# Attention of a hybrid layer, reordered: one turn holds both heads of a pair and one query tile, heaviest tile first

## What is computed

```python
for blk in range(S // Q_BLOCK):
    t0 = blk * Q_BLOCK
    L = t0 + Q_BLOCK
    z = jnp.einsum('bhqd,bhkd->bhqk', qb, kb) * scale          # kb, vb: the first L rows
    mask = s_idx < t_idx
    log_keep = jnp.where(mask, jax.nn.log_sigmoid(-z), 0.0)
    suffix = lax.cumsum(shifted, axis=3, reverse=True)         # shifted: log_keep one to the left
    A = jnp.where(mask, jnp.exp(jax.nn.log_sigmoid(z) + suffix), 0.0)
    outs.append(jnp.einsum('bhqk,bhkd->bhqd', A, vb))
```

## Time and profile before

| | us |
|---|---|
| median of 3 runs | 1343.46 (1341.79 to 1344.67) |
| the profiled execution, its span | 1344.4 |
| attention stage in it | 116.0 to 546.6 |
| PE busy in 116 to 546 | 393.2 of 430 |
| DVE busy there | 200.1 |
| ACT busy there | 187.6 |

### The profile page before, as it was taken

How to read it: one execution, slowest core, us unless ns; L and a number is a source line. 1 busy time by engine, 2 the same in 40 slices (tenths; PEclk the granted TensorE clock), 3 DMA queues, 4 the chain that set the end, 5 groups by cost and what they waited for, 6 DMA issues and landing times. The chain is left out here.

```text
span 1344.4 us, 16647 instructions
## 1 busy us (share of the span) xinstructions
PE 1196.3 (89%) x5806; PEld 968.3 (72%) x5806; DVE 870.1 (65%) x910; ACT 732.0 (54%) x918; POOL 146.7 (11%) x193
## 2 busy tenths in 40 slices
PE   5999979969989997899837999999999999999930
PEld 4887767747767775688716888888888888888820
DVE  4414444435435453723166999999999999999926
ACT  4322534543454236211206888888888888888810
POOL 1000000000000003100010111111111111111000
PEclk9999989979999999899857999999999999999975
DMA  6111100100000003611155999999999999999409
GB/s 203 37 32 32 32 16 16 32 16 17 16 16 23 28 14 125 265 49 48 39 249 196 357 389 384 381 382 380 384 384 385 382 386 378 384 384 388 174 17 374
DMA packets 57338, 261.88 MB, mean 195 GB/s; under 512 B 13008, under 2 KB 33488, under 8 KB 43984
## 3 DMA queue, kind: packets, MB, share of 16 engines
q1 hardware_dynamic: 46928, 240.31, 46.9%
q0 software_dynamic: 9216, 16.80, 3.3%
q10 hardware_dynamic: 1152, 4.19, 0.8%
HBM read 252.88 MB, written 25.17 MB: 207 GB/s over the span
## 5 line engine op out<-in xcount | busy, mean ns | idle before, releaser
L1250 DVE TENSOR_TENSOR e_lo<-W,e_hi 128x1024 fp32r<-128x1024 f32 x384 | 452.6, 1221 | 25.6 <-ACT e_hi L1244 22.5
L1244 ACT ACTIVATE e_hi<-W 128x1024 fp32r<-128x1024 f32 x384 | 403.3, 1060 | 96.8 <-PE ps L1215 94.0
L735 DVE TENSOR_TENSOR_SCAN kept<-kept,start_at 128x128 f32<-128x128 f32 (+7 forms) x64 | 88.7, 1385 | 210.7 <-ACT kept L587 177.6
L1213 PE MATMUL ps<-e_hi,xT_hi 128*128 128x512 f32 x512 | 204.2, 399 | 7.1 <-DVE e_lo L1250 7.1
L1215 PE MATMUL ps<-e_lo,xT_hi 128*128 128x512 f32 x512 | 201.5, 394 | 0.0
L1214 PE MATMUL ps<-e_hi,xT_lo 128*128 128x512 f32 x512 | 201.0, 393 | 0.0
L406 PE MATMUL ps<-xnT_hi,w_hi 128*128 128x512 f32 x320 | 128.4, 401 | 15.2 <-DVE u L699 7.1
L586 ACT ACTIVATE soft<-ps,q_scale 128x127 f32<-128x127 f32 (+7 forms) x54 | 38.0, 704 | 186.4 <-PE ps L454 175.6
L406 PE MATMUL ps<-xnT_hi,w_lo 128*128 128x512 f32 x320 | 127.9, 400 | 0.0
L406 PE MATMUL ps<-xnT_lo,w_hi 128*128 128x512 f32 x320 | 127.7, 399 | 0.0
L1213 PEld LDWEIGHTS ps<-e_hi,xT_hi 128*128 128x128 f32 x512 | 97.6, 191 | 27.0 <-issue 4.0
(11 more groups left out here) (207 smaller groups left out, 1768.2 us busy)
## 6 DMA issues: line engine op xcount, KB each, us to landing
W<-in_w_dram SPq DMA_DIRECT2D x96, 2048.0 KB, 10.7
w_raw<-in_w_in_dram SPq DMA_DIRECT2D x20, 512.0 KB, 4.0
yy<-y_rows SPq DMA_DIRECT2D x8, 1024.0 KB, 13.6
xt<-in_x_dram SPq DMA_DIRECT2D x8, 512.0 KB, 3.8
w_out_raw<-in_w_out_dram SPq DMA_DIRECT2D x4, 1024.0 KB, 9.4
xn_rows<-xn SPq DMA_DIRECT2D x8, 512.0 KB, 2.6
out_dram<-x ACTq DMA_DIRECT2D x8, 512.0 KB, 9.0
x<-in_x_dram SPq DMA_DIRECT2D x1, 3072.0 KB, 14.9
```

What stands on the lines that cost most here:

```text
L735: dve.tensor_tensor_scan(back, back, one[:, ::-1], 0.0, ALU.mult, ALU.max).then_inc(multiplied, 1)
L1213: pe.matmul(o, xs_hi[:, k], e_hi[:, p, cols], start=(k == 0), stop=False)
L1244: act.activation(e_hi[:, p], flat[:, p * D:(p + 1) * D], ACT.Copy).then_inc(s["hi_made"], 1)
L1250: dve.tensor_tensor(e_lo[:, p], flat[:, p * D:(p + 1) * D], e_hi[:, p], ALU.subtract).then_inc(s["lo_made"], 1)
```

## The change

A unit becomes both heads of a pair and one query tile, so there are 32 units instead of 64, and within a pair the tile falls from 7 to 0. `scores` issues each of the three products for head 0 and head 1 in turn, into different PSUM banks; `values` issues each key tile's product for head 0 and head 1 in turn, into the two halves of the partitions of one bank. `probsT` gets a buffer for each head. `turn`, `open_unit`, `take_turned` and `weigh` take the head as an argument; PE runs turn(n, 0), a first share of projection, turn(n, 1), a second share. `open_unit` makes `kept` first, and the scan waits for that alone. Scores have two banks for each head (four), transposes two, value products bank 6, and projection groups after the first eight all use bank 7: a group starts when the group before has been read. DVE, not ACT, copies the "c" groups. The shares are 8 and 16 ticks in each unit of the first three pairs, and 24 and 24 in the first four units of the last, none in its last four. JOIN is unit 4 of 8 (5 in the last pair), and the scores of the unit after stand ahead of it.

```diff
-SHARE = (11, 11, 11, 11, 11, 11, 11, 11, 11, 20, 20, 11, 11, 11, 10, 10)
-SHARE_LAST = (16,) * 12 + (0,) * 4
+SHARE = ((8, 16),) * 8
+SHARE_LAST = ((24, 24),) * 4 + ((0, 0),) * 4
...
+        group_bank = lambda g: 6 + g % 2 if g < PRE_GROUPS else 7
-        JOIN = (9, 9, 9, 13)
-        length = lambda n: (n % PU // 2 + 1) * P
+        JOIN = (4, 4, 4, 5)
+        tile_of = lambda n: NT - 1 - n % NT
+        length = lambda n: (tile_of(n) + 1) * P
-        Z = lambda use: ps[:, use % 3]
-        TB = lambda g: ps[:, 3 + g % 2]
-        VB = 5
+        Z = lambda use, h: ps[:, 2 * h + use % 2]
+        TB = lambda g: ps[:, 4 + g % 2]
+        VB = 6
...
                 def project(first, last):
-                            if g >= 2:
+                            if PRE_GROUPS <= g:
+                                pe.wait_ge(bank_read[(g - 1) % 2], (g - 1) // 2 + 1)
+                            elif g >= 2:
                                 pe.wait_ge(bank_read[g % 2], g // 2)
...
                 def scores(n):
-                        pe.matmul(z, q_hi[p % 2][rows, cols], k_hi[p % 2][rows, c0:c1], start=True, stop=False)
-                        pe.matmul(z, q_hi[p % 2][rows, cols], k_lo[p % 2][rows, c0:c1], start=False, stop=False)
-                        mm = pe.matmul(z, q_lo[p % 2][rows, cols], k_hi[p % 2][rows, c0:c1], start=False, stop=True)
+                        pe.wait_ge(z_read, z_done[z_first[n] + hf - 2])
+                        for i, (qs, ks) in enumerate(((0, 0), (0, 1), (1, 0))):
+                            for h in range(2):
+                                rows = slice(h * HD, (h + 1) * HD)
+                                mm = pe.matmul(Z(z_first[n] + hf, h)[:, 0:c1 - c0], q2[qs][rows, cols], k2[ks][rows, c0:c1],
+                                               start=(i == 0), stop=(i == 2))
...
                 def values(n):
                     for j in range(t + 1):
-                        mm = pe.matmul(ps[h * HD:(h + 1) * HD, VB, (t % 4) * P:(t % 4 + 1) * P], v[:, j, head], probsT[:, j, :],
-                                       start=(j == 0), stop=(j == t))
+                        for h in range(2):
+                            head = slice((2 * p + h) * HD, (2 * p + h + 1) * HD)
+                            mm = pe.matmul(ps[h * HD:(h + 1) * HD, VB, (t % 4) * P:(t % 4 + 1) * P], v[:, j, head], probsT[h][:, j, :],
+                                           start=(j == 0), stop=(j == t))
...
                 for n in range(UNITS):
-                    p, r = divmod(n, PU)
-                    if r != JOIN[p] + 1 and n + 1 < UNITS:
+                    p, r = divmod(n, NT)
+                    if n + 1 < UNITS:
                         scores(n + 1)
-                    if n >= 2:
-                        values(n - 2)
                     if n:
-                        turn(n - 1)
-                    project(ticks_by(n - 1), ticks_by(n))
-                    if r == JOIN[p] and p + 1 < NPAIR:
-                        sums_of_qk(p + 1)
-                    if r == JOIN[p] + 1:
+                        values(n - 1)
+                    turn(n, 0)
+                    project(ticks_by(n, 0), ticks_by(n, 1))
+                    turn(n, 1)
+                    if r == JOIN[p]:
+                        if p + 1 < NPAIR:
+                            sums_of_qk(p + 1)
                         if p:
                             sums_of_rows(p)
-                        scores(n + 1)
+                    project(ticks_by(n, 1), ticks_by(n, 2))
...
                 def open_unit(n, h):
+                    act.activation(kept[h][:, S - L:], z, ACT.Sigmoid, scale=down).then_inc(kept_made, 1)
+                    act.activation(soft[h][:, S - L:S - 1], z[:, 0:L - 1], ACT.Sigmoid, scale=up).then_inc(z_read, halves(n))
...
+                    for h in range(2):
+                        take_turned(n, h)
+                        if n + 1 < UNITS:
+                            open_unit(n + 1, h)
```

More of the change, by code:

```diff
@@ L260, in hymba_moe_layer, with share, ticks_by @@
-        halves = lambda n: (length(n) + BANK - 1) // BANK
[L261 to L265, removed]
+        UNITS = NPAIR * NT
+        PRE_GROUPS = 2 * PRE
+        def share(n):
+            return (SHARE if n < UNITS - NT else SHARE_LAST)[n % NT]
+        def ticks_by(n, part):
+            return PRE_GROUPS * TICKS + sum(sum(share(m)) for m in range(n)) + sum(share(n)[:part])
@@ L266, in hymba_moe_layer @@
+        z_first, z_before, sum_qk, sum_rows, z_done = {}, {}, {0: 0}, {}, [1, 3]
+        for n in range(UNITS):
+            z_first[n], z_before[n] = len(z_done), z_done[-1]
+            z_done += [z_done[-1] + 2 * halves(n)] * halves(n)
+            p, r = divmod(n - 1, NT)
+            if n and r == JOIN[p]:
                 if p + 1 < NPAIR:
-                    sum_qk[p + 1] = z_uses
-                    z_uses += 3
+                    sum_qk[p + 1] = len(z_done)
+                    z_done += [z_done[-1] + 1, z_done[-1] + 3]
@@ L269, in hymba_moe_layer @@
                 if p:
[L270 to L274, removed]
[L275 to L281 removed]
+                    sum_rows[p] = len(z_done)
@@ L282, in hymba_moe_layer @@
+                    for _ in joint_rows[p]:
+                        z_done.append(z_done[-1] + 2)
+        Z = lambda use, h: ps[:, 2 * h + use % 2]
+        z_reads = lambda n, h: z_before[n] + (h + 1) * halves(n)
+        assert all(z_first[n] % 2 == 0 for n in range(UNITS) if halves(n) == 2)
+        th = lambda n, h: sum(2 * halves(m) for m in range(n)) + h * halves(n)
+        TB = lambda g: ps[:, 4 + g % 2]
+        VB = 6
         row_gain = lambda r: gain_conv[:, r:r + 1] if r < CB else gain_attn[:, r - CB:r - CB + 1]
@@ new lines, in scores @@
+                    for hf in range(halves(n)):
+                        c0, c1 = hf * BANK, min((hf + 1) * BANK, length(n))
+                        pe.wait_ge(z_read, z_done[z_first[n] + hf - 2])
[4 more added lines that the diff above has]
+                                               start=(i == 0), stop=(i == 2))
@@ L475, in _ @@
                 sums_of_qk(0)
[L476 removed]
+                project(5 * TICKS, PRE_GROUPS * TICKS)
                 pe.wait_ge(v_read, NT)
@@ L623, in _ @@
                 v_out(NT - 1)
-                for g in range(5):
+                for g in range(4):
                     take(g)
@@ L763, in _ @@
                 chunk_lo(3)
+                take(4)
                 scale_keys(0)
-                for g in range(4, 6):
-                    take(g)
+                take(5)
                 keys_lo(0)
```

203 lines of the change are left out of this document (93 added, 110 removed).

## The result

The changed kernel takes 1245.88 us in the median of four runs (1243.80 to 1248.69); the kernel before takes 1344.01 beside it. The ratio is 0.9269, 95% interval 0.9254 to 0.9284.

A forecast was written before the change was run, and what follows sets the result against it. The prediction took PE to bound the stage: 307.7 us of work, 34.2 idle and 8 for the clock make 350 instead of 430, 80 less, so 1264 us for the kernel, range 1247 to 1300.

The forecast's parts named there:

- the sum: PE's work in the stage from first score to last value copy: 377.4 us before, 307.7 after the change.
- Scores: 26.3 forecast: Score products of two heads, in different row halves, run together; their 52.6 us of PE fall by 26.3.
- Value products: 31.4 forecast: Value products of two heads, in different column halves, run together; their 62.8 us of PE fall by 31.4.
- one pair costs one: Two heads' products side by side take the time of one; taken as 26.3 us saved for scores, 31.4 for values.
- the row for two row halves: Profile row of the kernel before: both heads' first scores in merged pairs, 0.28 to 0.34 us long, like one alone.
- The load at 281.44: Head 0's weight load behind a join, ahead of head 1's 281.62 product; cited against strict program order for two row groups.
- Changes of kind: PE's extra time between kinds of product, about 0.50 us a unit: 32 us before, 12 saved by 32 units.
- the waits at the joins: PE idle at the joins for the open unit, table and Ln, and DVE's late copies: 14.6 of 34.2 us idle.
- table and Ln: PE waits at the joins for the open unit and ACT's table and Ln: 0.8, 2.4 and 2.4 us.
- DVE's copy of a projection group: In the second and third pair, key work, row scalings and head 1's scan delay it; PE waits about 4.5 us each.
- half clock: PE's loss to the granted clock in the stage: 8 us instead of 15.8, as fewer long gaps precede dense work.
- The end: Behind the last projection, tiles 3 to 0 are left: 26 us instead of 39, PE idle for 13 of them.

The follow-up runs named there:

- the three loads: The changed kernel with two more table loads at each join, 2.57 us of ACT each time; 1257.58 us, 0.9353 of the kernel before.

## Why the prediction was right and wrong

**PE's work: right.** PE's busy time at half clock, 5.02 us from 119 to 126 and 2.70 from 436 to 446, would be half of that at full clock, so half clock cost 3.9 us; 311.7 busy less 3.9 is 307.8, and the sum said 307.7. Scores: 26.3 forecast, 23.9 come back when pairing is taken away. Value products: 31.4 forecast, 29.5. Both bounds' choice of "one pair costs one" came out, and the row for two row halves carried over to two column halves; no row had shown the second, so it was a guess with a chance of its own against it. (Scores as priced add up to 52.3 us, not 52.6; it changes nothing.)

The tiling page's "Up to 2×" ("TensorEngine Tiling (Array Packing)", Theoretical Speedup, in the Trainium skill) agrees: 3.71 against 1.97 us. The rule of the Trainium skill's page "TensorE: Matmul & The Clock Gate", Part 3, that products start strictly in order and loads pass only in another row group, does not hold here: value products that share all rows pair in full, and by head they still pair at the seam. The load at 281.44 that the prediction set against this rule is no counterexample, since the rule lets a load of another row group pass; but the row above it does show one. Its x2 from 281.39 lasts 0.55 us, so it holds the product of that load, 0.49 long, from some 281.45 on, ahead of the products at 281.50 and 281.62 that come before it in the program.

**Changes of kind: right.** The unit above has 0.50 of them, and a second turn adds 0.08 (a first projection row of 0.47 instead of 0.39); 32 * 0.58 = 18.6 for the 20 in the sum.

**The step that failed: the waits at the joins.** I put 14.6 of the 34.2 us of idle time there. All idle time is 20.3, of which the start has 5.0 (4.22, 0.20, 0.54; forecast 6.6) and the end 12.6 (forecast 13), so joins and all between have 2.7. Two things were wrong in it. First, I had PE wait 2.4 us for table and Ln at the second and third join. At the second, ACT needs 3.6 us from PE's last transposes to the end of the Ln of q, and PE's own sums of q and k fill the same 3.6 (241.72 to 245.32). The prediction prices these sums rightly in PE's work (16 * 0.11 and 4 * 0.43, 3.5 us); it does not set them in full against the wait.

Second, I had PE wait 4.5 us for DVE's copy of a projection group in each of the second and third pair. The queue ahead of that copy stands there as I said it would. The changed kernel behind the second join, DVE, then PE's first projection product behind the next unit's transposes:

```profile
258.20 1.28 DVE L734 SCALAR_TENSOR_TENSOR y_mix<-y_mix,gain_attn 128x1024 f32<-128x1024 f32 x1
...
260.59 0.69 DVE L744 TENSOR_TENSOR_SCAN kept<-kept,start_at 128x256 f32<-128x256 f32 x1
...
261.66 0.69 DVE L708 TENSOR_TENSOR u<-ps,u 128x512 f32<-128x512 f32 x1
...
262.49 0.47 PE L417 MATMUL ps<-xnT_hi,w_hi 128*128 128x512 f32 x1
```

The copy is done at 262.35, and PE, which has the scores, value products and transposes of the next unit until 262.49, does not wait; the copy comes 0.14 us before it is needed. DVE can start that queue at 253.7 because it was free before: PE's sums make the group end later and the scores ahead of the join are open early, so DVE idles 7.5 us before the copy at 253.06. With the scores behind the sums, as in the old order, that earlier copy is late and PE waits.

**The clock.** I took 8 us for half clock and it is 3.9: with no wait over 0.7 us from 126 to 420, PE stays at 2.4 GHz from 126 to 436. The idle time (13.9 less than forecast) and the clock (4.1) are the 18 us by which the time was missed. They are tied: the three loads add 5.1 us of waits at two joins and 3.4 of clock behind them. Not every wait does it: the one of 2.65 us before 423.99 in the changed kernel left the clock at 1.00 (420 to 430).

**The end: right.** 26 us forecast behind the last projection, 28 measured. W_out's rounding, 10.3 us long, ends 15 us behind the last projection, off the path as said.

```profile
422.70 10.27 POOL L376 CAST w_out_hi<-w_out_raw 128x1024 fp32r<-128x1024 f32 x8 [30.48 <-DMA w_out_raw<-in_w_out_dram]
```

**The range.** Its low end of 1247 let the waits fall by 15 us and kept the clock's 8 nearly whole. It should have let both fall together: 1264 - 14.6 - 4 is 1245.

## What to carry to other kernels

Two products that use different halves of the array, by rows or by columns, cost as much as one where they follow closely: for the scores, in threes, no alternation was needed; for the value products, in runs of up to eight, it gave two thirds of the gain (19.2 of 29.5 us). When the order of units is free, put the ones with a long chain through other engines where other PE work still fills the gaps, and the light ones last. Before pricing a wait, count what the waiting engine itself has to do until then, and price a wait that disappears together with the half clock that stood behind it.

## What the runs showed of the hardware

PE started a product ahead of its turn when it used the other half of the columns, though both need all 128 rows: sixteen passes of head 0 and sixteen of head 1 in sequence took 3.33 us instead of 3.71, and three scores of each head paired in full without being alternated (0.7 us of difference in the stage). A pair costs 0.109 us for two value passes and 0.24 for two scores of 512 columns, the same as one. Half clock appeared in the changed kernel only with PE's two long idle stretches, 4.2 us before 120.8 (0.51 from 119 to 126) and 4.4 before 438.9 (0.53 from 436 to 446), and in no stretch between, where PE is busy 301.4 of 310 us. A float32 product with v stands in the records as two passes (576 for 288 products), and the three table loads at a join follow each other at 1.28 us.
